# A routing stage's one-hot rows shared out anew, and the next stage's first splits and weights made at its end

## The reference, cut to what matters

```python
def peer_ffn(x, w_query, keys_1, keys_2, expert_down, expert_up):
    q = (x @ w_query).reshape(b, s, PEER_HEADS, 2, PEER_HALF)      # 8 heads
    s1, s2 = scores of the two halves against 128 keys each
    v1, i1 = lax.top_k(s1, 16);  v2, i2 = lax.top_k(s2, 16)
    cand = v1[..., :, None] + v2[..., None, :];  idx = i1 * 128 + i2
    top_score, pos = lax.top_k(cand, 16);  experts = idx at pos
    gates = softmax(top_score)
    act = gelu(x . expert_down[experts], exact)
    y = sum over heads and k of gates * act * expert_up[experts]
```

## Time and profile before

| | |
|---|---|
| median of three runs | 3178.79 us |
| profiled execution, its own time | 3169.57 us |
| its span, first to last instruction | 3167.9 us |
| mean granted TensorE clock | 0.973 |
| busy in the span: TensorE, its weight loads | 94%, 76% |
| busy: VectorE, ScalarE, GpSimd | 68%, 40%, 17% |
| the four token tiles of the routing stage | about 871 to 1138 us |
| the three expert blocks behind them | 1138 to 1155 us |

### The profile page before, as it was taken

How to read it: one execution, slowest core, us unless ns; L and a number is a source line. 1 busy time by engine, 2 the same in 40 slices (tenths; PEclk the granted TensorE clock), 3 DMA queues, 4 the chain that set the end, 5 groups by cost and what they waited for, 6 DMA issues and landing times. The chain is left out here.

```text
span 3167.9 us, 42380 instructions
## 1 busy us (share of the span) xinstructions
PE 2985.1 (94%) x14292; PEld 2422.8 (76%) x14292; DVE 2139.6 (68%) x4227; ACT 1282.2 (40%) x1960; POOL 526.8 (17%) x664
## 2 busy tenths in 40 slices
PE   7999999988988889999999999999998899989997
PEld 5678876877777777788888888888877677856886
DVE  5574435346788958888888888888883682545333
ACT  4443343223355642344444444444444332455222
POOL 1023450003477740000000000000001030034000
PEclk8999999999999999999999999999999999989998
DMA  2220002322233354444333334443332212200331
GB/s 105 74 67 28 21 24 94 107 93 98 83 140 140 137 213 135 133 133 132 128 121 124 123 126 132 132 126 124 124 130 80 74 41 67 93 1 12 122 95 72
DMA packets 138195, 317.01 MB, mean 100 GB/s; under 512 B 9296, under 2 KB 74960, under 8 KB 135888
## 3 DMA queue, kind: packets, MB, share of 16 engines
q1 hardware_dynamic: 135440, 281.38, 27.5%
q10 hardware_dynamic: 2624, 33.93, 2.6%
HBM read 275.43 MB, written 39.85 MB: 100 GB/s over the span
## 5 line engine op out<-in xcount | busy, mean ns | idle before, releaser
L197 DVE TENSOR_TENSOR split<-raw,split 128x1024 fp32r<-128x1024 f32 x172 | 209.7, 1226 | 435.0 <-ACT split L188 434.6
L188 ACT ACTIVATE split<-raw 128x1024 fp32r<-128x1024 f32 x220 | 231.5, 1058 | 637.6 <-PE merge L214 193.0
L2172 PE MATMUL up<-up_high,weight_high 128*128 128x512 f32 x700 | 272.3, 389 | 0.0
L2173 PE MATMUL up<-up_low,weight_high 128*128 128x512 f32 x700 | 272.3, 389 | 0.0
L2174 PE MATMUL up<-up_high,weight_low 128*128 128x512 f32 x700 | 272.3, 389 | 0.0
L365 POOL TENSOR_TENSOR xl<-col,xh 128x512 fp32r<-128x512 f32 x8 | 10.0, 1271 | 1073.1 <-ACT xh L337 1073.1
L1867 POOL TENSOR_SCALAR hot<-count,second 128x128 f32<-128x128 f32 x256 | 172.7, 689 | 36.8 <-PE score L1748 25.7
L1748 PEld LDWEIGHTS score<-hot,hot 128*128 128x128 f32 x1024 | 135.1, 200 | 54.9 <-POOL hot L1867 31.2
L1748 PE MATMUL score<-hot,hot 128*128 128x128 f32 x1024 | 142.9, 288 | 34.3 <-POOL hot L1867 19.1
L1918 DVE TENSOR_SCALAR hot<-count,first,gate 128x128 f32<-128x128 f32 x512 | 172.9, 401 | 0.0
L2301 PE MATMUL dt<-xh,split 128*128 128x512 f32 x416 | 162.0, 390 | 1.8 <-ACTq L2419 1.8
(11 more groups left out here) (510 smaller groups left out, 7859.9 us busy)
## 6 DMA issues: line engine op xcount, KB each, us to landing
raw<-in_stream SPq DMA_DIRECT2D x440, 512.0 KB, 3.6
gates<-stage ACTq DMA_DIRECT2D x16, 2048.0 KB, 6.7
gate<-gates SPq DMA_DIRECT2D x32, 1024.0 KB, 8.0
h<-in_x SPq DMA_DIRECT2D x4, 512.0 KB, 6.1
h<-in_x SPq DMA_DIRECT2D x1, 2048.0 KB, 8.5
h_saved<-h SPq DMA_DIRECT2D x1, 2048.0 KB, 7.5
h<-h_saved SPq DMA_DIRECT2D x1, 2048.0 KB, 14.2
rows<-h SPq DMA_DIRECT2D x4, 512.0 KB, 2.6
```

Source lines behind the costliest of these rows:

```text
L188: act.activation(g.high[t % slots], g.raw[:, t % RAW, :], ACT.Copy).then_inc(g.high_split, 1)
L197: dve.tensor_tensor(g.low[t % slots], g.raw[:, t % RAW, :], g.high[t % slots], ALU.subtract).then_inc(g.low_split, 1)
L2172: pe.matmul(bank, wh, uh, start=start, stop=False, skip_group_check=True)
L2173: pe.matmul(bank, wh, ul, start=False, stop=False, skip_group_check=True)
```

## The change

In words:

- VectorE makes all four plain rows of a quad with one `tensor_tensor` comparison of two broadcast inputs, and two gated rows instead of four.
- GpSimd makes one gated row instead of two plain ones, a `tensor_scalar` with two operations.
- ScalarE makes the last gated row instead of a plain one, as relu(gate - gate * |first - count|), with `less` = -gate made once a token tile. TensorE waits for four makers instead of three.
- SPREAD becomes (4, 4, 2, 2), so four expert blocks lie behind the last quad instead of three. They use four slots for split tiles. ScalarE and VectorE (not GpSimd) split them and the first three tiles of the next stage there.
- ScalarE, not SyncE, issues the load of the first gates, after the first of these four blocks; SyncE waits for one of the two stores only and then loads `h`.
- The weights of blocks 0 and 1 are made in `peer_route` by VectorE and ScalarE; `peer_early` starts with weights 2 and 3 and one split.

The core of the diff:

```diff
-SPREAD = (4, 4, 3, 2)
+SPREAD = (4, 4, 2, 2)
...
+    less = g.at("less", R + 56.5, [P, P])
...
-    FIRST, BY_POOL = 3, 2
+    FIRST, BY_VECTOR = 3, 2
...
+    early_buffers(g)
...
-                for s in range(2):
-                    sp.wait_ge(stored[s], 16 * S // GROUP // 2)
-
-                sp.dma_start(g.gate[:, :, :, :], g.gates[:, :, 0:4, :].rearrange("n p e t -> p n e t"))\
-                  .then_inc(g.first_gates, 16)
+                sp.wait_ge(stored[1], 16 * S // GROUP // 2)
                 sp.dma_start(g.h[:, :, :], saved).then_inc(g.rows_back, 16)
...
-                    last = mm_columns(g, pe, base + N_QUERY + j, down[j % 3][:, :], start=c, stop=c + 1)
+                    last = mm_columns(g, pe, base + N_QUERY + j, down[j % 3][:, :], start=c, stop=c + 1,
+                                      slots=2 if j < n_spread else 4)
...
-                    pe.wait_ge(third_made, n + 1)
+                    pe.wait_ge(pool_made, n + 1)
+                    pe.wait_ge(act_made, n + 1)
...
+                def negate(t):
+
+                    act.activation(less[:, :], gate[:, t * P:t * P + P], ACT.Copy, scale=-1.0).then_inc(negated, 1)
...
-                    act.activation(hot2[:, n % 4, QUAD - 1, :], count[:, :], ACT.Abs, scale=-1.0,
-                                   bias=second[:, t:t + 1]).then_inc(apart, 1)
+                    act.activation(hot1[:, n % 4, QUAD - 1, :], count[:, :], ACT.Abs, scale=-1.0,
+                                   bias=first[:, t:t + 1]).then_inc(apart, 1)
...
-                    act.activation(hot, hot, ACT.Relu, scale=-1.0, bias=1.0).then_inc(third_made, 1)
+                    act.activation(hot, hot, ACT.Relu, scale=less[:, t % P:t % P + 1],
+                                   bias=gate[:, t:t + 1]).then_inc(act_made, 1)
...
                 for j in range(n_spread, EARLY):
-                    down_done(j)
+                    if j == n_spread:
+
+                        act.wait_ge(product, QUADS)
+                        for k in range(2, 4):
+                            split_high(g, act, 0, N_QUERY + j + k, 4)
+                    tile_done(g, act, 0, N_QUERY + j)
+                    act.activation(g.early[:, j, :], down[j % 3][:, :], ACT.Gelu).then_inc(activated, 1)
+                    if j < EARLY - 1:
+                        split_high(g, act, 0, N_QUERY + j + 4, 4)
+                    if j == n_spread:
+                        for s in range(2):
+                            act.wait_ge(stored[s], 16 * S // GROUP // 2)
+
+                        act.dma_start(g.gate[:, :, :, :], g.gates[:, :, 0:4, :].rearrange("n p e t -> p n e t"))\
+                           .then_inc(g.first_gates, 16)
+                    if j == EARLY - 2:
+                        for e in range(2):
+                            act.wait_ge(weighed, e + 1)
+                            act.activation(g.early_wh[:, e, :], g.early_w[:, e, :], ACT.Copy).then_inc(w_high, 1)
...
-                    for k in range(BY_POOL):
-                        at = n * QUAD + k
-                        ins = pool.tensor_scalar(hot2[:, n % 4, k, :], count[:, :], second[:, at:at + 1], None,
-                                                 ALU.is_equal)
-                    ins.then_inc(second_made, 1)
+                    at = n * QUAD + BY_VECTOR
+                    pool.tensor_scalar(hot1[:, n % 4, BY_VECTOR, :], count[:, :], first[:, at:at + 1],
+                                       gate[:, at:at + 1], ALU.is_equal, ALU.mult).then_inc(pool_made, 1)
...
-                for j in range(n_spread, EARLY):
-                    low(j)
-
...
-                    for k in range(QUAD):
+                    at = slice(n * QUAD, n * QUAD + QUAD)
+                    dve.tensor_tensor(hot2[:, n % 4, :, :], count[:, :].unsqueeze(1).to_broadcast([P, QUAD, N_KEYS]),
+                                      second[:, at].unsqueeze(2).to_broadcast([P, QUAD, N_KEYS]),
+                                      ALU.is_equal).then_inc(second_made, 1)
+                    for k in range(BY_VECTOR):
...
+                dve.wait_ge(product, QUADS)
+                for k in range(n_spread + 2, EARLY + 2):
+                    low(k)
+                dve.wait_ge(g.first_gates, 16)
+                for e in range(2):
+                    dve.tensor_tensor(g.early_w[:, e, :].rearrange("p (n t) -> p n t", t=GROUP),
+                                      g.early[:, e, :].rearrange("p (n t) -> p n t", t=GROUP),
+                                      g.gate[:, :, e, :], ALU.mult).then_inc(weighed, 1)
+                    dve.wait_ge(w_high, e + 1)
+                    dve.tensor_tensor(g.early_wl[:, e, :], g.early_w[:, e, :], g.early_wh[:, e, :], ALU.subtract)
+                low(EARLY + 2)
...
-                for j in range(B):
-                    if j == 0:
-                        split_high(g, act, 0, 2, SL)
-                        split_high(g, act, 0, 3, SL)
+                split_high(g, act, 0, 3, SL)
+                act.sem_inc(w_high, 2)
+                for j in range(2, B):
                     high(0, j)
...
-                dve.sem_inc(weighed, 1)
-                split_low(g, dve, 0, 2, SL)
+                dve.sem_inc(weighed, 3)
+                dve.sem_inc(w_low, 2)
+                for j in range(2, B):
+                    weights(0, j)
                 split_low(g, dve, 0, 3, SL)
-                dve.wait_ge(g.first_gates, 16)
-                for j in range(B):
-                    weights(0, j)
```

More of the change, by code:

```diff
@@ L202, in tile_done, with mm_columns @@
     eng.wait_ge(g.tile_used, i + (g.base + j + 3))
-def mm_columns(g, pe, t, out, chunks=DC, x=None, start=0, stop=None):
+def mm_columns(g, pe, t, out, chunks=DC, x=None, start=0, stop=None, slots=2):
     xh, xl = x or (g.xh, g.xl)
-    hi, lo = g.high[t % 2], g.low[t % 2]
+    hi, lo = g.high[t % slots], g.low[t % slots]
     for c in range(start, stop or chunks):
@@ L1658, in peer_route @@
     saved = nc.dram_tensor("h_saved", [S, D], F32, kind="Internal").ap().rearrange("(t p) d -> p t d", p=P)
-    FIRST, BY_POOL = 3, 2
+    FIRST, BY_VECTOR = 3, 2
     per_half, per_pick, steps_of = 5 * TT, 5 * HEADS, 13
     done_at, n_spread = tiles_done()
+    assert n_spread == EARLY - 4 and (base + N_QUERY + n_spread) % 4 == 0
+    early_buffers(g)
     (passed, pool_passed, act_passed, q_read, scored, s_read, key_picked, key_kept, counted, summed, picked, step, grown,
-     chosen_made, turned, kept, activated, second_made, first_made, third_made, apart, product, read, h_saved) = (
+     chosen_made, turned, kept, activated, second_made, first_made, pool_made, act_made, apart, negated, product, read, h_saved) = (
         g.sem(x) for x in (
@@ L1667, in peer_route @@
             "counted", "summed", "picked", "pick_step", "exp_done", "chosen", "turned", "kept", "activated", "second_hot",
-            "first_hot", "second_hot_by_act", "apart", "product", "read", "h_saved"))
+            "first_hot", "first_hot_by_pool", "first_hot_by_act", "apart", "negated",
+            "product", "read", "h_saved"))
+    weighed, w_high = g.sem("weighed"), g.sem("w_high")
     stored = [g.sem(f"stored{s}") for s in range(2)]
@@ L1789, in grow @@
                     act.activation(res[:, :], res[:, :], ACT.Exp).then_inc(grown, 1)
+                def negate(t):
+                    act.activation(less[:, :], gate[:, t * P:t * P + P], ACT.Copy, scale=-1.0).then_inc(negated, 1)
                 def distance(n):
                     t = n * QUAD + QUAD - 1
-                    act.activation(hot2[:, n % 4, QUAD - 1, :], count[:, :], ACT.Abs, scale=-1.0,
-                                   bias=second[:, t:t + 1]).then_inc(apart, 1)
+                    act.activation(hot1[:, n % 4, QUAD - 1, :], count[:, :], ACT.Abs, scale=-1.0,
+                                   bias=first[:, t:t + 1]).then_inc(apart, 1)
                 def last_row(n):
+                    act.wait_ge(negated, n // PER_TILE + 1)
                     act.wait_ge(apart, n + 1)
-                    hot = hot2[:, n % 4, QUAD - 1, :]
-                    act.activation(hot, hot, ACT.Relu, scale=-1.0, bias=1.0).then_inc(third_made, 1)
+                    t = n * QUAD + QUAD - 1
+                    hot = hot1[:, n % 4, QUAD - 1, :]
+                    act.activation(hot, hot, ACT.Relu, scale=less[:, t % P:t % P + 1],
+                                   bias=gate[:, t:t + 1]).then_inc(act_made, 1)
                 act.sem_inc(activated, 3)
@@ L1814, in _ @@
                         act.wait_ge(product, t * PER_TILE)
+                        act.wait_ge(act_made, t * PER_TILE)
+                    negate(t)
                     for q in range(4):
@@ L1919, in rows @@
                                                 gate[:, at:at + 1], ALU.is_equal, ALU.mult)
[L1920 to L1923, removed]
                     ins.then_inc(first_made, 1)
@@ L2017, in _, with low @@
                     rows(TT)
```

(11 more changed lines are left out.)

## The result

The changed kernel takes 3155.73 us (median; 3151.22 to 3165.32), the kernel before 3178.73 us in the same comparison. The ratio is 0.9941 (95% interval 0.9924 to 0.9959): 23 us faster. The forecast was 3159.5 us with a range of 3152 to 3176. A second comparison, with 15 executions of the kernel before, gave 3154.75 against 3176.42 us, ratio 0.9932 (0.9905 to 0.9958).

A forecast was written before the change was run, and what follows sets the result against it. VectorE's own chain of work was taken to set a tile's length. Terms -10.8 - 2.1 - 0.5 - 1.0 + 5.4 - 10.3 = -19.3 us off the 3178.8 us median gave 3159.5 us, range 3152 to 3176.

The forecast's parts named there:

- tiles 0 to 2: Routing tiles 0 to 2: cheaper VectorE quads -10.8 us, one GpSimd low split fewer -2.1, shorter burst -0.5.
- tile 3: Last routing tile: with GpSimd and VectorE relieved, TensorE sets the end, -1.0 us.
- expert tile moved behind: Eight chunks moved from tile 2 to behind the quads cost 5.4 us in full there.
- handover: Start of the next stage: cost falls from 15.0 to 4.6 to 4.7 us, so -10.3 (-11.3 to -6).
- there only the first counts: Last five quads of a tile, paced by TensorE at 1.59 us each: VectorE's saving counts once, 0.1 us.
- Rival (3): GpSimd's gated row costs twice a plain one, 1.65 us a quad: sum -2.9, 3175.9 us; chance 0.06.
- rival (4): VectorE's comparison waits each time for GpSimd's row, on average 0.3 us a quad: +19, 3198 us; chance 0.08.
- Rival (1): TensorE's own pace sets tiles 0 to 2, so VectorE's gain is lost: -11.3, 3167.5 us; chance 0.12.
- With both relieved TensorE sets the end: Tile 3: with GpSimd and VectorE less busy, TensorE's own 40.0 us decides, where 42.8 was taken.
- 1.7 us of half clock and the 0.4 us remain: Tile 3: clock loss and the negation's delay stay on top of TensorE's 40.0 us, leaving -1.0 us.
- T+19: Handover: gates land 19 us after the last product at T, between T+16.0 and T+22.2, sharing engines with h.
- rival (2): Handover: gates come late, hole 6.2 us and 2.8 us of clock: handover -6.0, sum -15.0, 3163.8 us; chance 0.10.

The follow-up runs named there:

- second profile: The changed kernel run once more, unaltered: 412.7 us from the copies that open tile 0 to the last matmul of the stage behind.
- the plain row for ScalarE: Kernel with low splits by VectorE, but in tile 3 ScalarE makes a plain row, VectorE compares three rows and makes three gated: 3138.07 against 3175.80 us.

## Why the prediction was right or wrong

The forecast of -19.3 us stands beside a local -16.0 and -20.1 and medians of -23.0 and -21.7. Part by part, with the first and the second profile of the changed kernel:

| | forecast | measured |
|---|---|---|
| tiles 0 to 2 | -10.8 - 2.1 - 0.5 = -13.4 | -16.5, -19.2 |
| tile 3 | -1.0 | +1.2, +0.2 |
| expert tile moved behind | +5.4 | +5.4, +5.4 |
| handover | -10.3 | -6.2, -6.5 |
| sum | -19.3 | -16.1, -20.1 |

(The handover's measured -6.2 is 12.23 - 6.87 = 5.4 us of hole and 0.8 of clock: the next stage lasts 136.5 us from TensorE's first matmul to its last before, 135.7 after. In the second profile it is 12.23 - 6.43 = 5.8 and 0.7.)

**Tiles 0 to 2: mechanism right, one term too small.** The comparison costs 0.60 us as estimated from the 128x448 one, and two gated rows 0.51 rather than 0.54, so a quad takes 1.11 us where it took 1.27: 0.16 less, not 0.13. Over a tile's quads without a stall the mean is 1.12 us where it was 1.28 to 1.31, so what the change saves is 0.16 to 0.18. This saving per quad is the term that was mis-sized. From the copies that open a tile to the first of its last five quads it took 61.1, 60.8 and 57.9 us, and now takes 56.3, 55.8 and 51.6 (56.1, 55.8 and 51.6 in the second profile): 16.2 to 16.3 us less, where 3 x 3.5 + 2.1 = 12.6 was forecast.

That "there only the first counts" in the last five quads was right. VectorE makes them 0.6 to 0.8 us faster in each tile, and waits the longer for it (at the end of tile 0 for 8.85 us instead of 7.90). TensorE is busy from there to the next copies, and how long it takes follows its granted clock. Tile 1 before, after, and in the second profile:

```profile
1007.28:1021.61 14.33, 14.33 (x100) 13.44 (x99) 6.32 (x26) 7.51 (x13) 4.75 (x5) 0.91 0.30 124
1005.95:1021.72 15.77, 15.77 (x99) 14.65 (x99) 5.71 (x17) 7.87 (x13) 4.13 (x3) 0.82 0.30 117
1000.55:1013.72 13.17, 13.13 (x97) 12.02 (x97) 5.66 (x17) 7.87 (x13) 4.54 (x3) 1.00 0.36 141
```

In tile 0 this part takes 14.4 us before and 14.5 in both profiles after. In tile 2 it falls from 13.6 to 11.8, with fewer chunks in it and the clock at 1.00 instead of 0.93. So the 2.6 us between the two profiles, and about 2 us of what the tiles gave beyond the forecast in the second, are clock. The moved tile saved 3.3 us of tile 2 where 2.6 was put.

**The rule on modes.** The Trainium skill (VectorE: DVE Perf Modes, the perf-mode tier table) has tensor_scalar at twice the speed of tensor_tensor in float32. For these rows the trace shows that this doesn't decide: 128 columns by tensor_scalar start the next after 0.19 to 0.22 us, 512 by tensor_tensor after 0.60, so four of the first cost 0.78 to 0.88 and lose to one of the second.

**GpSimd and VectorE.** GpSimd's gated row has a mean of 1.13 us, as the 1.15 taken. Rival (3) needed 1.65 and rival (4) a comparison that waits; neither came. With the low splits it is the other way round and VectorE pays, as the earlier trace rows had it. One of tile 0 in the changed kernel shows it again (VectorE's two gated rows take 2.65 us where 0.59 is usual):

```profile
887.33 2.54 POOL L197 TENSOR_TENSOR split<-raw,split 128x1024 fp32r<-128x1024 f32 x1 [2.02 <-ACT split L188]
...
887.56 2.65 DVE L1948 TENSOR_SCALAR hot<-count,first,gate 128x128 f32<-128x128 f32 x2
```

The prediction priced such a stall rightly but only counted the one that the change takes away. The kernel with the splits on VectorE shows what the others are worth: 11.6 us of the four tiles (248.5 to 236.9).

**Rival (1), TensorE binds the tiles**, didn't come for the change: the tiles fell by more than the forecast, and VectorE waited for a product 13 times, 3.3 us in all, 12 of them in tile 3. But TensorE does set the last 12 to 16 us of each tile, and its clock counts in full there.

**Tile 3.** TensorE sets it, as forecast and as the plain row for ScalarE confirms, but the gain wasn't there. The tile starts with a hole of 2.87 us instead of 2.52, the 0.3 to 0.4 us put down for the negation, and the clock of the tile is 0.93 in the first profile where it was 0.96.

```profile
1087.88 3.76 PE L1751 MATMUL score<-hot,hot 128*128 128x128 f32 x16 [2.87 <-ACT hot L1809]
...
1114.60 2.66 DVE L1948 TENSOR_SCALAR hot<-count,first,gate 128x128 f32<-128x128 f32 x2
1117.96 1.13 PE L1751 MATMUL score<-hot,hot 128*128 128x128 f32 x8 [1.53 <-DVE hot L1943]
```

The last two rows show what the forecast left out. The kernel before has such a wait too:

```profile
1124.48 1.13 PE L1748 MATMUL score<-hot,hot 128*128 128x128 f32 x8 [1.56 <-POOL hot L1867]
```

"With both relieved TensorE sets the end" holds but for the one low split that GpSimd still makes in this tile: it stops VectorE, and TensorE waits 1.53 us for VectorE's rows, as it waited 1.56 for GpSimd's before. With that split on VectorE the wait is gone and the tile takes 44.3 us, although at a clock of 0.92. In the second profile, at 0.96, it took 45.4. That "1.7 us of half clock and the 0.4 us remain" was an assumption that didn't hold in each execution.

**Handover: the step that failed.** The moved work lies where it was put: ScalarE issues the reload 7.6 us behind the last product (forecast 7.9), the last chunk and four tiles end at 22.4 (22.5), and from the gates' landing to TensorE's next matmul it takes 6.6 us (6.4). What failed is the landing itself, T+19 in the forecast with T+22.2 as its end:

```profile
1138.81 0.44 ACTq L1872 DMA_DIRECT2D gate<-gates  x1
1139.35 0.69 SPq L1690 DMA_DIRECT2D h<-h_saved  x1
...
1154.25 0.69 DVE L2055 TENSOR_TENSOR weight<-early,gate 128x512 f32<-128x512 f32 x1 [8.24 <-DMA gate<-gates]
...
1158.24 1.22 DVE L197 TENSOR_TENSOR split<-raw,split 128x1024 fp32r<-128x1024 f32 x1
1160.82 0.79 PE L1367 MATMUL up<-split,weight_high 128*128 128x512 f32 x1 [6.87 <-DVEq L2192]
```

T is 1131.2, so the gates are there at T+23.0: the reload of 1 MB took 15.4 us, not the 8.0 of the earlier trace rows. I had taken the middle of "alone" and "both share". The 1 MB of gates, issued 0.54 us ahead of the 2 MB of h, landed about a microsecond behind them: neither its head start nor its smaller size helped it. This is rival (2), given a chance of 0.10, whose -6.0 us for the handover is close to the -6.2 and -6.5 measured. Held apart, the load took 9.6 us, the gates landed at T+17.3 and TensorE's hole was 1.98 us: close to the near ends that the prediction had for both (T+16.0 and 2.0).

That the total came out near the forecast is luck, since errors cancel: the tiles gave 3.1 to 5.8 us more, handover and tile 3 together 5.0 to 6.3 less.

## What to carry to other kernels

Where many small rows are made, count starts: one broadcast comparison of 512 columns (0.60 us) beat four of 128 (0.78 to 0.88) in the mode that is called faster. Where an engine's time is lost to another's instruction, price the work on the engine that suffers: here VectorE made the splits itself in 1.2 us and got back the 2.1 that a split on GpSimd had cost it. A load that someone waits for is better issued alone, with the one that nobody needs yet held behind it; if both are under way, expect the first to land about when both have. Where one engine makes a row of small instructions and another follows, ask for each part of the tile which of the two is behind: a saving in the part that the other engine paces is worth nothing.

## What the runs showed of the hardware

- GpSimd's 128x1024 split with two inputs stops one VectorE instruction for all of its time (2.65 us where two rows take 0.59); VectorE's 128x512 comparison with two inputs isn't lengthened by GpSimd's one-input row (697 ns with, 710 without), and lengthens that row instead: 0.79 us at the least, mean 1.13. The Trainium skill (GPSIMD Engine Reference, Key points) says that GpSimd contends with VectorE's instructions that have two SBUF inputs or are in a 2-port perf mode; the prediction used the first half only. The trace agrees that there is contention, and adds that it isn't symmetric. VectorE's one-input rows lengthen GpSimd's row nearly as much (mean 1.05); whether they ran in such a mode isn't shown here.
- Two loads at a time, of 1 and 2 MB, took 15.4 and 13.8 us; one behind the other 9.6 and 7.7, with three weight tiles of 512 KB issued just ahead in both kernels.
- ScalarE's Relu of 128x128 with scale and bias from memory starts the next after 0.386 us, without them after 0.20. That is twice the 0.1 I had added; ScalarE hid it, busy 50.4 of 70.8 us.
- Without any edit the same code took up to 9.6 us more in one execution than in another ahead of tile 0, and up to 9.3 behind the changed stages, as the granted clock fell to 0.50 in other places. A single profile of this kernel can't show a difference of 10 us in its span; a stretch around the change can.
